# Fetching tile by tile with the second selection beside, and every second expert row summed on TensorE

## The chip, the cores and the metric

The kernel runs on one core of a Trainium2 chip. The metric is the device time of one execution in microseconds. A core has TensorE (PE), VectorE (DVE), ScalarE (ACT), GpSimd (POOL) and SyncE (SP), each with its own instruction stream; they meet by semaphores. DMAs are issued from SP's queue and from POOL's, and run on 16 DMA engines.

## The reference

Two blocks of two layers each on 256 tokens of width 1024. The change concerns the expert layer of the second block, which is called three times: in layer 0 for two streams of 256 tokens, in layer 1 for one.

```python
def _peer(h, wq, keys, u, v):              # per chunk of 128 tokens
    q = (hb @ wq).reshape(tc, 8, 2, 128)
    s = einsum('thpk,hpnk->thpn', q, keys)
    s_top, i_top = lax.top_k(s, 16)                    # per head and half: 16 of 128 keys
    cand = s_top[:, :, 0, :, None] + s_top[:, :, 1, None, :]
    cid = i_top[:, :, 0, :, None] * 128 + i_top[:, :, 1, None, :]
    best, pos = lax.top_k(cand.reshape(tc, 8, -1), 16) # 16 of 256 candidates per head
    eid = take_along_axis(cid.reshape(tc, 8, -1), pos, -1)
    g = softmax(best, -1)
    act = gelu(einsum('td,thed->the', hb, u[eid]))
    return einsum('the,thed->td', g * act, v[eid])
```

So each token chooses 8 x 16 = 128 experts out of 16384. Of each it needs one row of u (1024 floats) for a score and one row of v for the weighted sum. Before each layer the stream is scaled and shifted by vectors that come from `silu(c) @ w_mod`; those of layer 1 depend on nothing of layer 0.

## The kernel before

The program is written as stages, one behind the other, each with its own buffers and semaphores and an all-engine barrier at its end. The order inside a stage is written out by hand, engine by engine. An expert layer (`peer`, L1732) has these:

- scaling, `token_rows` (L1634) and `best_keys` (L1440): queries, key scores and the 16 best keys per head and half, for two tiles of 128 tokens (a token per partition).
- `select_experts` (L1544), once per tile: DVE forms the 256 candidates per head (`cand`, L1604), finds the 16 best by max, max_index and match_replace (`best16`, L1422), and turns positions into expert numbers through comparisons with 0 to 15 (`hit`, L1616 to L1620, twice). ACT does the exponentials (L1587). DVE ends with the weights (L1622 to L1625) and the index (L1628). Beside it, in layer 0 only, `Conditioning` (L502) computes a part of layer 1's scale and shift vectors: SP loads 1 MB pieces of `w_mod` into a ring of three (L521), PE multiplies (L539), ACT copies each group's row out (L527), PE turns the rows (L544), DVE adds the bias (L550). Three groups of two pieces go beside each selection, twelve groups in all.
- `gathered_experts` (L1654): POOL fetches for slot e and tile i one uv row per token (u and v side by side, 8 KB for each of 128 partitions, 1 MB in all) with an indirect DMA (L1676) into a ring of 12 buffers. The items alternate between the two tiles: 128 slots x 2 tiles = 256 fetches. They are worked off in batches of four. DVE multiplies and reduces the u half to a score (L1685), ACT applies gelu to four scores (L1721), DVE multiplies them by the weights (L1692), and then adds the four v halves, scaled by that number, to the tile's sum (L1699 for the first, L1703). The sums of a batch stand behind the scores of the next. A buffer is free when its sum is done (`s_summed`), and POOL waits for that before the fetch that reuses it. At the end PE turns both tiles' sums (L1728) and DVE adds them, gated, to x (L1715).

In what follows a fetch is one such item, and a stage's fetches are numbered from 0.

## Time and profile before

| | us |
|---|---|
| median of 3 runs | 4422.59 (4412.22 to 4424.36) |
| profiled execution, its own time | 4426.39 |
| its span in the trace | 4424.6 |
| DVE busy | 3183.9 (72%) |
| PE busy | 1744.0 (39%) |
| POOL busy | 1341.5 (30%) |
| ACT busy | 797.7 (18%) |
| DMA, software queue (the fetches) | 110592 packets, 805.36 MB |
| DMA, SP's queue | 58176 packets, 255.33 MB |

The profile comes from one execution. Its span leaves out 1.8 us of the execution's own time. Busy shares are means over very different stages: the three fetch stages run from 1712.9 to 2376, 2522.9 to 3186 and 3735.9 to 4398 us; PE is idle in them and busy in the stages between. A value in a fetch stage is therefore read from windows inside it. "Idle before, releaser" is the time in which the engine stood still ahead of an instruction, and what ended it.

### The profile page before, as it was taken

To read this page: it belongs to the slowest core of one execution; us is meant where nothing else is said; L and a number is where in the kernel's file an instruction comes from. 1 tells how busy PE (TensorE), PEld (TensorE's weight loads), DVE (VectorE), ACT (ScalarE), POOL (GpSimd) and SP (SyncE) were. 2 spreads that over 40 slices of the span, in tenths; PEclk is the share of its full clock that TensorE was granted. 3 is DMA by queue.
4 is the path that set the end of the run, shared out by engine and by line. 5 is a ranking of instruction groups with operands and counts; after the bars stand their busy time and mean duration, and the time that the engine had idled before them with its cause. 6 is when DMAs were issued, how large, how long until landed. Compare 5 with 4: busy or idle time off the path is not lost. (4 is left out here: it accounts for less than half of the span.)

```text
span 4424.6 us, 32217 instructions
## 1 busy us (share of the span) xinstructions
PE 1744.0 (39%) x9324; PEld 1322.3 (30%) x9324; DVE 3183.9 (72%) x5368; ACT 797.7 (18%) x1477; POOL 1341.5 (30%) x820
## 2 busy tenths in 40 slices
PE   6768975987877863000004500000166571000001
PEld 1657925954635650000004200000054471000001
DVE  3546545645264368999997799999843657999997
ACT  1335413522232230000002100000032240000000
POOL 0000000000000032666664166666300031666663
PEclk9868987998985786555556755555587885555555
DMA  7214452544100137999995499999630032999996
GB/s 285 80 38 151 162 228 100 176 168 174 56 0 1 38 122 286 421 419 418 417 419 210 186 422 422 418 418 415 261 125 0 1 124 87 422 422 419 419 418 251
DMA packets 168890, 1062.02 MB, mean 240 GB/s; under 512 B 18604, under 2 KB 22444, under 8 KB 57664
## 3 DMA queue, kind: packets, MB, share of 16 engines
q0 software_dynamic: 110592, 805.36, 43.9%
q1 hardware_dynamic: 58176, 255.33, 16.3%
q8 instruction: 41, 0.67, 0.1%
q14 instruction: 81, 0.66, 0.0%
HBM read 1059.56 MB, written 1.05 MB: 240 GB/s over the span
## 5 line engine op out<-in xcount | busy, mean ns | idle before, releaser
L1676 POOL DMA_INDIRECT peer_gather_raw<-in_peer_uv,peer_experts x768 | 1226.9, 1598 | 922.0 <-DVE peer_gather_out L1703 473.2
L1685 DVE CUSTOM_DVE_ANT_0 peer_gather_raw<-peer_gather_raw,peer_rows 128x1024 f32<-128x1024 f32 x768 | 912.0, 1223 | 122.8 <-DMA peer_gather_raw<-in_peer_uv,peer_experts 122.7
L1703 DVE SCALAR_TENSOR_TENSOR peer_gather_out<-peer_gather_raw,peer_gather_gelu,peer_gather_out 128x1024 f32<-128x1024 f32 x762 | 928.3, 1280 | 6.8
L1728 PE MATMUL peer_gather_acc<-all_constants,peer_gather_out 128*128 128x128 f32 x48 | 11.0, 424 | 2049.9 <-DVE peer_gather_out L1703 2049.9
L1540 POOL TENSOR_TENSOR peer_keys_lo<-peer_pick_wq_raw,peer_keys_hi 128x1024 fp32r<-128x1024 f32 x48 | 114.3, 2387 | 2107.5 <-ACT peer_keys_hi L1499 2107.5
L1728 PEld LDWEIGHTS peer_gather_acc<-all_constants,peer_gather_out 128*128 128x128 f32 x48 | 9.8, 227 | 2050.2 <-DVE peer_gather_out L1703 2050.2
L1721 ACT ACTIVATE peer_gather_gelu<-peer_gather_score 128x4 f32<-128x4 f32 x192 | 39.4, 205 | 1900.1 <-DVE peer_gather_score L1685 1900.1
L124 PE MATMUL ffn_up_acc<-first_h_hi,ffn_up_hi 128*128 128x256 f32 x704 | 202.1, 287 | 36.9 <-DVE ffn_up_lo L642 36.9
L124 PE MATMUL ffn_up_acc<-first_h_lo,ffn_up_hi 128*128 128x256 f32 x704 | 201.6, 286 | 0.0
L124 PE MATMUL ffn_up_acc<-first_h_hi,ffn_up_lo 128*128 128x256 f32 x704 | 201.5, 286 | 0.0
L452 PE MATMUL mod_acc<-mod_weights,mod_act_c 128*1 128x512 f32 (+1 forms) x288 | 142.0, 640 | 46.7 <-DMA mod_weights<-in_ada_w 32.9
L124 PEld LDWEIGHTS ffn_up_acc<-first_h_hi,ffn_up_hi 128*128 128x128 f32 x704 | 137.7, 196 | 37.7 <-DVE ffn_up_lo L642 37.7
L124 PEld LDWEIGHTS ffn_up_acc<-first_h_lo,ffn_up_hi 128*128 128x128 f32 x704 | 137.8, 196 | 0.0
L124 PEld LDWEIGHTS ffn_up_acc<-first_h_hi,ffn_up_lo 128*128 128x128 f32 x704 | 137.6, 196 | 0.0
L124 PE MATMUL peer_keys_acc<-peer_pick_hi,peer_keys_hi 128*128 128x256 f32 x384 | 115.5, 301 | 17.4 <-POOL peer_keys_lo L1540 17.4
L124 PE MATMUL peer_keys_acc<-peer_pick_lo,peer_keys_hi 128*128 128x256 f32 x384 | 111.4, 290 | 0.0
L124 PE MATMUL peer_keys_acc<-peer_pick_hi,peer_keys_lo 128*128 128x256 f32 x384 | 111.3, 290 | 0.0
L489 DVE SCALAR_TENSOR_TENSOR mod_part_sum<-mod_weights,mod_act_c,mod_part_sum 128x512 f32<-128x512 f32 x144 | 105.0, 750 | 3.8
L642 DVE TENSOR_TENSOR ffn_up_lo<-in_up_raw,ffn_up_hi 128x1024 fp32r<-128x1024 f32 x88 | 103.8, 1219 | 4.9 <-ACT ffn_up_hi L601 4.8
L539 PE MATMUL peer_select_next_acc<-peer_select_next_raw,peer_select_next_silu 128*2 128x512 f32 x192 | 90.1, 632 | 40.4 <-DMA peer_select_next_raw<-in_w_mod 40.4
L124 PE MATMUL ffn_down_acc<-ffn_hidden_hi,ffn_down_hi 128*128 128x256 f32 x352 | 101.6, 288 | 11.1 <-DVE ffn_down_lo L215 11.1
L124 PE MATMUL ffn_down_acc<-ffn_hidden_lo,ffn_down_hi 128*128 128x256 f32 x352 | 101.2, 287 | 0.0
(481 smaller groups left out, 4884.8 us busy)
## 6 DMA issues: line engine op xcount, KB each, us to landing
mod_weights<-in_ada_w SPq DMA_DIRECT2D x48, 1024.0 KB, 7.7
in_up_raw<-in_w_up SPq DMA_DIRECT2D x88, 512.0 KB, 4.1
mod_weights<-in_w_mod SPq DMA_DIRECT2D x24, 1024.0 KB, 6.2
peer_pick_wq_raw<-in_peer_wq SPq DMA_DIRECT2D x48, 512.0 KB, 3.5
peer_select_next_raw<-in_w_mod SPq DMA_DIRECT2D x24, 1024.0 KB, 5.8
...
peer_gather_raw<-in_peer_uv,peer_experts POOLq DMA_INDIRECT x768, 11.2
...
```

Of the source, the lines that this page charges most:

```text
L124: ins = nc.tensor.matmul(out, a, b, start=start and n == 0, stop=stop and n == 2, skip_group_check=True)
L452: ins = nc.tensor.matmul(acc[0:n, g % 2, :], act_c[:, k, :], wt[:, 2 * (g % 2), k, :], start=(k == 0), stop=False)
L489: ins = nc.vector.scalar_tensor_tensor(mine, wt[:, slot, k, :], scale, mine, ALU.mult, ALU.add)
L539: ins = nc.tensor.matmul(self.acc[0:n, g % 2, :], self.silu[:, i * KD // 2 + k, :], self.raw[:, u % 3, k, :], start=(i == 0 and k == 0), s ...
L642: nc.vector.tensor_tensor(w[1][:, slot, :], raw[:, slot, :], w[0][:, slot, :].bitcast(F32), ALU.subtract).then_inc(s_lo, 1)
L1540: nc.gpsimd.tensor_tensor(w[1][:, m % 4, :], raw[:, m % 4, :], w[0][:, m % 4, :].bitcast(F32), ALU.subtract).then_inc(s_lo, 1)
L1676: nc.gpsimd.indirect_dma_start(raw[:, n % ring].rearrange("p c d -> p (c d)"), None, uv_rows, bass.IndirectOffsetOnAxis(index[:, i, e:e + ...
L1685: nc.vector.tensor_tensor_reduce(raw[:, n % ring, 0, :], raw[:, n % ring, 0, :], rows[:, i, :], 1.0, 0.0, ALU.mult, ALU.add, score[:, e, i ...
L1703: nc.vector.scalar_tensor_tensor(out[:, i, :], raw[:, n % ring, 1, :], gelu[:, e, i:i + 1], out[:, i, :], ALU.mult, ALU.add).then_inc(s_su ...
L1721: nc.scalar.activation(flat(gelu, b), flat(score, b), ACT.Gelu).then_inc(s_gelu, 1)
L1728: ins = nc.tensor.transpose(acc[:, k, i * P:(i + 1) * P], out[:, i, k * P:(k + 1) * P], ident)
```

## The change

The two selections and the fetch stage become one stage, `fetched_experts`. Only the first tile's selection is done ahead of the fetches. The second tile's is a Python generator, `side`, of which DVE takes one step behind each of the first 20 scores. The fetches go tile by tile: 128 of tile 0, then 128 of tile 1. They are worked off in batches of two. The even fetch's v half is summed on PE: ACT writes a 128x128 diagonal with the token's factor (L1758), and PE multiplies it with the 1024 columns of v in two matmuls of 512 that accumulate in PSUM over the tile (L1792). The odd fetch's v half is summed on DVE as before (L1691, L1694). At the end of a tile DVE adds the two partial sums (`take`), PE turns the result (`turn`) and DVE adds it to x (`add`); for tile 0 this happens while tile 1's fetches run. POOL waits for PE's semaphore ahead of even fetches and for DVE's ahead of odd ones. `Conditioning` has six groups in place of three and runs once per stream instead of once per tile.

```diff
 class Conditioning:
-    GROUPS = 3
+    GROUPS = 6
...
+def fetched_experts(nc, name, rows, top, where, uv_rows, x, gate, iota, ident, upcoming=None):
+        batch, ring, dring = 2, 12, 4
+        per_tile = slots // batch
+        batches = NT * per_tile
+        n_of = lambda i, e: i * slots + e
...
             def _(pool):
-                for n, (e, i) in enumerate(items):
-                    if n >= ring:
-                        pool.wait_ge(s_summed, n - ring + 1)
...
+                for i in range(NT):
+                    pool.wait_ge(s_chosen, 2 * i + 1)
+                    for e in range(slots):
+                        n = n_of(i, e)
+                        if n >= ring:
+                            pool.wait_ge(s_summed if e % 2 == 0 else s_half, (n - ring) // 2 + 1)
+                        nc.gpsimd.indirect_dma_start(raw[:, n % ring].rearrange("p c d -> p (c d)"), None, uv_rows,
+                                                     bass.IndirectOffsetOnAxis(index[:, i, e:e + 1], 0)).then_inc(s_landed[n % ring], 16)
...
+                def select(tile):
...
+                    yield
+                    for h in range(PEER_H):
+                        step.done(nc.vector.max(best[:, h, 0:8], cand[:, h, :]))
+                        if h % 4 == 3:
+                            yield
+                    step.wait()
+                    for h in range(PEER_H):
+                        step.done(nc.vector.max_index(pos[:, h, 0:8], best[:, h, 0:8], cand[:, h, :]))
+                        step.done(nc.vector.match_replace(cand2[:, h, :], best[:, h, 0:8], cand[:, h, :], float(-3.4e38)))
+                        if h % 2 == 1:
+                            yield
...
+                    nc.vector.scalar_tensor_tensor(index[:, tile, :], pick[:, 0, :], float(N_KEYS), pick[:, 1, :],
+                                                   ALU.mult, ALU.add).then_inc(s_chosen, 1)
+                    dve.wait_ge(s_exp, 2 * tile + 2)
...
+                def accumulate(b):
+                    i, e = b // per_tile, b % per_tile * batch + 1
...
+                        dve.wait_ge(s_half, n // 2)
+                        nc.vector.scalar_tensor_tensor(odd[:], raw[:, n % ring, 1, :], gelu[:, i, e:e + 1], odd[:],
+                                                       ALU.mult, ALU.add).then_inc(s_half, 1)
+                def take(i):
+                    dve.wait_ge(s_half, (i + 1) * slots // 2)
+                    dve.wait_ge(s_summed, (i + 1) * slots // 2)
...
+                    nc.vector.tensor_tensor(out[:], summed[:, i].rearrange("p b c -> p (b c)"), odd[:], ALU.add).then_inc(s_out, 1)
+                def scores(b, side):
+                    i = b // per_tile
+                    for e in range(b % per_tile * batch, (b % per_tile + 1) * batch):
+                        if b and e % batch == 1:
+                            weigh(b - 1)
+                            accumulate(b - 1)
+                        n = n_of(i, e)
                         dve.wait_ge(s_landed[n % ring], 16 * (n // ring + 1))
...
+                        next(side, None)
...
+                for _ in select(0):
+                    pass
+                side = select(1)
+                scores(0, side)
                 for b in range(1, batches):
+                    scores(b, side)
+                    if b == 24 and beside:
+                        beside.vector(dve)
+                    if b == per_tile:
+                        take(0)
+                    if b == per_tile + 12:
+                        add(0)
...
             def _(act):
+                def spread(b):
+                    act.wait_ge(s_weighted, b + 1)
...
+                    nc.scalar.activation(diag[:, b % dring, :], ident, ACT.Copy, scale=gelu[:, i, e:e + 1]).then_inc(s_diag, 1)
+                if beside:
+                    beside.scalar(act, 0, 3)
+                exponentials(0)
+                if beside:
+                    beside.scalar(act, 3, beside.GROUPS)
+                activate(0)
+                for b in range(1, batches):
+                    activate(b)
+                    if b == 6:
+                        exponentials(1)
+                    spread(b - 1)
...
             def _(pe):
+                if beside:
+                    beside.tensor(pe)
                 for i in range(NT):
+                    for e in range(0, slots, 2):
+                        n = n_of(i, e)
+                        pe.wait_ge(s_diag, n // 2 + 1)
+                        for half in range(2):
+                            ins = nc.tensor.matmul(summed[:, i, half, :], diag[:, n // 2 % dring, :], raw[:, n % ring, 1, half * 512:(half + 1) * 512],
+                                                   start=(e == 0), stop=(e == slots - 2))
+                        ins.then_inc(s_summed, 1)
+                        if i and e == 16:
+                            turn(0)
```

Where the order changes, row by row. A semaphore is printed under the name of its first user in the program, so names such as `mod0_silu` say only that there is a wait. First VectorE (DVE) before, at the end of tile 1's selection in layer 0 and the start of the fetch stage:

```order
L1620 TENSOR_REDUCE peer_select_pick<-peer_select_hit 128x128 [waits mod0_silu]
L1622 TENSOR_REDUCE peer_select_total<-peer_select_best 128x8 [waits mod0_row,mod0_silu]
L1623 RECIPROCAL peer_select_total<-peer_select_total 128x8 [waits mod0_silu]
L1625 TENSOR_TENSOR peer_share<-peer_select_best,peer_select_total 128x128 [waits mod0_silu]
L1628 SCALAR_TENSOR_TENSOR peer_experts<-peer_select_pick 128x128
L550 TENSOR_TENSOR second_mods<-peer_select_next_cols,all_vectors 128x24 [waits swa_attention_out]
L556 TENSOR_SCALAR second_mods<-second_mods 128x8 [waits ffn0_up_silu]
L1565 UNCONDITIONAL_BRANCH
L1679 UNCONDITIONAL_BRANCH [waits barrier_Pool_Activation_PE_DVE_SP_release]
L1685 ISA peer_gather_raw,peer_gather_score<-peer_gather_raw,peer_rows 128x1024 [waits load_all_loaded]
L1685 ISA peer_gather_score 128x1
```

Here the scores (the custom instruction, L1685) stand behind both selections, behind the conditioning's two rows and behind a barrier.

VectorE now, at the end of tile 0's selection (the last pick is L1666, the index L1668, the weights L1671 to L1673):

```order
L1666 TENSOR_REDUCE peer_fetch_pick<-peer_fetch_hit 128x128 [waits mod0_joined]
L1668 SCALAR_TENSOR_TENSOR peer_fetch_experts<-peer_fetch_pick 128x128 [waits mod0_joined]
L1671 TENSOR_REDUCE peer_fetch_total<-peer_fetch_best 128x8 [waits swa_attention_back]
L1672 RECIPROCAL peer_fetch_total<-peer_fetch_total 128x8 [waits mod0_joined]
L1673 TENSOR_TENSOR peer_fetch_share<-peer_fetch_best,peer_fetch_total 128x128 [waits mod0_joined]
L1713 ISA peer_fetch_raw,peer_fetch_score<-peer_fetch_raw,peer_rows 128x1024 [waits load_all_loaded,swa_attention_out]
L1713 ISA peer_fetch_score 128x1
L1623 CAST peer_fetch_key_no<-peer_index 128x256
L1624 CAST peer_fetch_ranks<-all_constants 128x16
L1628 TENSOR_TENSOR peer_fetch_cand<-peer_top 128x2048
L1713 ISA peer_fetch_raw,peer_fetch_score<-peer_fetch_raw,peer_rows 128x1024 [waits mod0_loaded1,mod0_joined]
```

The index moved ahead of the weights; behind it comes the first score, and the rows of tile 1's selection (L1623 on) stand between the scores.

POOL before, from the end of the keys to the fetches:

```order
L1540 TENSOR_TENSOR peer_keys_lo<-peer_pick_wq_raw,peer_keys_hi 128x1024 [waits mod0_used] x16
L1457 UNCONDITIONAL_BRANCH
L49 ISA [waits barrier_Pool_Activation_PE_DVE_SP_gather] x4
L1671 UNCONDITIONAL_BRANCH [waits barrier_Pool_Activation_PE_DVE_SP_gather]
L1676 DMA peer_gather_raw<-in_peer_uv,peer_experts 128x2048 x12
L1676 DMA peer_gather_raw<-in_peer_uv,peer_experts 128x2048 [waits ffn0_up_silu] x244
```

POOL now:

```order
L1542 TENSOR_TENSOR peer_keys_lo<-peer_pick_wq_raw,peer_keys_hi 128x1024 [waits mod0_used] x16
L1459 UNCONDITIONAL_BRANCH
L49 ISA [waits barrier_Pool_Activation_PE_DVE_SP_gather] x2
L1605 UNCONDITIONAL_BRANCH [waits barrier_Pool_Activation_PE_DVE_SP_gather]
L1613 DMA peer_fetch_raw<-in_peer_uv,peer_fetch_experts 128x2048 [waits swa_attention_out]
L1613 DMA peer_fetch_raw<-in_peer_uv,peer_fetch_experts 128x2048 x11
L1613 DMA peer_fetch_raw<-in_peer_uv,peer_fetch_experts 128x2048 [waits peer00_fetch_summed]
L1613 DMA peer_fetch_raw<-in_peer_uv,peer_fetch_experts 128x2048 [waits peer00_fetch_half]
```

The first fetch waits for the index and for no barrier of the selections; later ones wait in turn for PE's and for DVE's sums.

ScalarE (ACT) now, from the conditioning to the first diagonals (L529 copies a group's row out, L1745 is the exponential, L1750 a gelu, L1758 a diagonal):

```order
L526 ACTIVATE peer_fetch_next_silu<-all_vectors 128x16
L529 ACTIVATE peer_fetch_next_rows<-peer_fetch_turned 2x512 [waits peer00_fetch_next_used] x3
L1745 ACT_TABLE_LOAD
L1745 ACTIVATE peer_fetch_best<-peer_fetch_best 128x128 [waits swa_attention_back]
L529 ACTIVATE peer_fetch_next_rows<-peer_fetch_turned 2x512 [waits peer00_fetch_next_used] x3
L1750 ACT_TABLE_LOAD
L1750 ACTIVATE peer_fetch_gelu<-peer_fetch_score 128x2 [waits ffn0_up_silu] x2
L1758 ACTIVATE peer_fetch_diag<-all_constants,peer_fetch_gelu 128x128 [waits ffn0_up_hidden_hi]
L1750 ACTIVATE peer_fetch_gelu<-peer_fetch_score 128x2 [waits ffn0_up_silu]
```

All six rows of the conditioning stand ahead of the first gelu; each diagonal stands behind the gelu of the next batch.

## Rows read from the trace of the kernel before

**Rows 1.** The page's costliest groups: busy us, mean ns, idle before and its releaser.

```profile
L1685 DVE CUSTOM_DVE_ANT_0 peer_gather_raw<-peer_gather_raw,peer_rows 128x1024 f32<-128x1024 f32 x768 | 912.0, 1223 | 122.8 <-DMA peer_gather_raw<-in_peer_uv,peer_experts 122.7
...
L1703 DVE SCALAR_TENSOR_TENSOR peer_gather_out<-peer_gather_raw,peer_gather_gelu,peer_gather_out 128x1024 f32<-128x1024 f32 x762 | 928.3, 1280 | 6.8
```

**Rows 2.** Windows: us, then busy of PE, PEld, DVE, ACT, POOL; clock, DMA share, GB/s.

```profile
1800.00:2300.00 500.00, 0.00 (x0) 0.00 (x0) 479.46 (x650) 10.27 (x50) 324.88 (x200) 0.50 1.01 419
```

**Rows 3.** Timeline of VectorE in mid-stage: start us, us, line, tiles, [idle <-releaser].

```profile
1806.37 1.22 DVE L1685 CUSTOM_DVE_ANT_0 peer_gather_raw<-peer_gather_raw,peer_rows 128x1024 f32<-128x1024 f32 x1 [0.31 <-DMA peer_gather_raw<-in_peer_uv,peer_experts]
...
1807.52 0.16 DVE L1692 TENSOR_TENSOR peer_gather_gelu<-peer_gather_gelu,peer_share 128x4 f32<-128x4 f32 x1
...
1816.33 1.23 DVE L1685 CUSTOM_DVE_ANT_0 peer_gather_raw<-peer_gather_raw,peer_rows 128x1024 f32<-128x1024 f32 x1 [0.23 <-DMA peer_gather_raw<-in_peer_uv,peer_experts]
```

**Rows 4.** Timeline of VectorE, first stage: first score, first products, 16th and last score.

```profile
1718.68 1.23 DVE L1685 CUSTOM_DVE_ANT_0 peer_gather_raw<-peer_gather_raw,peer_rows 128x1024 f32<-128x1024 f32 x1 [7.74 <-DMA peer_gather_raw<-in_peer_uv,peer_experts]
...
1738.08 1.42 DVE L1699 TENSOR_SCALAR peer_gather_out<-peer_gather_raw,peer_gather_gelu 128x1024 f32<-128x1024 f32 x2
...
1756.63 1.23 DVE L1685 CUSTOM_DVE_ANT_0 peer_gather_raw<-peer_gather_raw,peer_rows 128x1024 f32<-128x1024 f32 x1 [0.29 <-DMA peer_gather_raw<-in_peer_uv,peer_experts]
...
2358.80 1.23 DVE L1685 CUSTOM_DVE_ANT_0 peer_gather_raw<-peer_gather_raw,peer_rows 128x1024 f32<-128x1024 f32 x1 [0.24 <-DMA peer_gather_raw<-in_peer_uv,peer_experts]
```

**Rows 5.** Timeline of ScalarE, first selection of layer 0.

```profile
1672.93 0.59 ACT L527 ACTIVATE peer_select_next_rows<-peer_select_next_acc 2x512 f32<-2x512 f32 x1 [6.28 <-PE peer_select_next_acc L539]
...
1674.83 0.31 ACT L1587 ACTIVATE peer_select_best<-peer_select_best 128x128 f32<-128x128 f32 x1
```

**Rows 6.** TensorE: timeline of a conditioning, windows of it and of a layer norm.

```profile
1650.80 22.09 PE L539 MATMUL peer_select_next_acc<-peer_select_next_raw,peer_select_next_silu 128*2 128x512 f32 x48 [11.29 <-DMA peer_select_next_raw<-in_w_mod]
...
1660.00:1673.00 13.00, 12.89 (x31) 2.38 (x28) 12.72 (x27) 0.66 (x2) 0.00 (x0) 1.00 0.45 161
...
3187.00:3192.00 5.00, 4.81 (x6) 2.19 (x7) 0.00 (x0) 0.00 (x0) 0.00 (x0) 0.50 0.00 0
```

**Rows 7.** Timeline of POOL: the stage's first fetch and four later ones.

```profile
1712.88 1.09 POOL L1676 DMA_INDIRECT peer_gather_raw<-in_peer_uv,peer_experts  x1 [80.22 <-SPq L1670]
...
1992.69 2.65 POOL L1676 DMA_INDIRECT peer_gather_raw<-in_peer_uv,peer_experts  x1 [0.89 <-DVE peer_gather_out L1703]
...
2341.86 1.74 POOL L1676 DMA_INDIRECT peer_gather_raw<-in_peer_uv,peer_experts  x1 [2.38 <-DVE peer_gather_out L1703]
...
2343.90 0.94 POOL L1676 DMA_INDIRECT peer_gather_raw<-in_peer_uv,peer_experts  x1 [0.30 <-issue]
...
2345.15 1.98 POOL L1676 DMA_INDIRECT peer_gather_raw<-in_peer_uv,peer_experts  x1 [0.30 <-issue]
```

**Rows 8.** Timeline of VectorE, first selection of layer 0.

```profile
1645.95 0.29 DVE L1598 CAST peer_select_key_no<-peer_pick_index 128x256 bf16<-128x256 uint32 x1 [0.90 <-PEq L50]
...
1651.30 0.09 DVE L1429 MATCH_VALUE_LOAD peer_select_pos<-peer_select_best,peer_select_cand 128x8 f32 x1
...
1674.38 2.29 DVE L1620 TENSOR_REDUCE peer_select_pick<-peer_select_hit 128x128 f32<-128x2048 bf16 x1
...
1677.47 0.28 DVE L1628 SCALAR_TENSOR_TENSOR peer_experts<-peer_select_pick 128x128 uint32<-128x128 f32 x1
```

**Rows 9.** Timeline of the first stage's end.

```profile
2365.12 4.87 DVE L1703 SCALAR_TENSOR_TENSOR peer_gather_out<-peer_gather_raw,peer_gather_gelu,peer_gather_out 128x1024 f32<-128x1024 f32 x4
...
2368.86 3.68 PE L1728 MATMUL peer_gather_acc<-all_constants,peer_gather_out 128*128 128x128 f32 x16 [660.86 <-DVE peer_gather_out L1703]
...
2372.57 3.23 DVE L1715 SCALAR_TENSOR_TENSOR all_x<-peer_gather_acc,second_mods,all_x 128x256 f32<-128x256 f32 x8 [2.57 <-PE peer_gather_acc L1728]
```

**Rows 10.** Timeline of layer 1: first index, first fetch, last score.

```profile
3701.31 0.28 DVE L1628 SCALAR_TENSOR_TENSOR peer_experts<-peer_select_pick 128x128 uint32<-128x128 f32 x1
...
3735.92 0.95 POOL L1676 DMA_INDIRECT peer_gather_raw<-in_peer_uv,peer_experts  x1 [79.44 <-SPq L1670]
...
4380.59 1.23 DVE L1685 CUSTOM_DVE_ANT_0 peer_gather_raw<-peer_gather_raw,peer_rows 128x1024 f32<-128x1024 f32 x1 [0.24 <-DMA peer_gather_raw<-in_peer_uv,peer_experts]
```

274 lines of the change are left out of this document (129 added, 145 removed).

## The prediction

> **What bounds the kernel now.** I read the page's slices first: three stretches of about 640 us stand at some 420 GB/s with the DMA digit at 9, and they are the three fetch stages, 256 fetches of 1 MB each. The rest of the span is not touched. Then the costliest groups [rows 1]: VectorE (DVE) carries two passes over each fetch, the score (1223 ns) and the sum (1280 ns), and had only 122.8 us in all before its scores, all of it spent waiting for a DMA. That makes it look as if DVE were nearly the bound. The windows decide it [rows 2]: over 500 us in the middle of a stage the DMA share is 1.01 at 419 GB/s, while DVE is busy 479 of 500 us. The batch rows say the same [rows 3]: four scores and four sums repeat every 9.96 us (1806.37 to 1816.33), or 2.49 us per fetch, and in each period DVE waits 0.2 to 0.3 us for a fetch and not the other way round. Over a whole stage a fetch costs 2.509 us: from the 16th score at 1756.63 to the last at 2358.80 are 602.2 us for 240 fetches [rows 4]. So a fetch stage is bound by the DMA engines, with DVE about 3% behind them. Taking work off DVE there can't by itself shorten it. What can be shortened is the time in which the DMA engines carry no fetch: the second selection ahead of each stage, and the tail behind it.
>
> **The sum on VectorE and TensorE.** Half of the 1280 ns sums leave DVE. A pair of fetches then costs it two scores (pitch 1.15 to 1.2 us with the accumulator read), one sum (1.2) and one small product (0.2 [rows 3]): 3.8 us against 5.02 us of DMA. In its place ScalarE makes a diagonal per pair (128x128; the nearest row is the 128x128 exponential, 0.31 us [rows 5]), and TensorE does two f32 matmuls of 512 columns. Such a matmul stands in the trace as two records (24 matmuls per selection in the code, x48 in the row [rows 6]). At granted clock 1.00 (2.4 GHz) the window holds 31 records in 13 us, 0.42 each; at 0.50 (1.2 GHz) it holds 6 in 5 us, 0.83 each [rows 6]. A pair costs TensorE 1.7 us at the upper and 3.3 us at the lower level, below 5.02 in both. The clock was 0.50 through the middle of the stage before, with TensorE idle [rows 2]; I take 3.3 and keep 1.7 as the other end. Cost on the path: nothing in steady state, hidden by the DMA. The cover holds if slots come free in time. An even slot is held from its landing until its matmuls end: 3 fetches (7.5) to the second score behind it, 1.2 for that, 0.05 assumed for the hand-over, 0.21 for a gelu (10.27 us for 50 [rows 2]) and 0.31 on ScalarE, 3.3 on TensorE, together 12.6 us with rounding up. A new fetch needs 5.8 us from issue to landing (1712.88 [rows 7] to 1718.68 [rows 4]). That is 18.4 of the ring's 12 x 2.49 = 29.9 us, so 11 us are spare. The merge in the middle (DVE waits for the last pair's matmuls, 4 us, and adds for 1.3) fits into these 11, and so does the addition of tile 0 to x. The gain is nothing here, the loss nothing; what DVE's spare 1.2 us per pair pays for is the next part.
>
> **The start of the fetches.** Before, the first is issued at 1712.88, behind both selections. Now it needs only the first index. That is computed right behind the second pick (1674.38 + 2.29 = 1676.7 [rows 8]), before the weights: 1676.7 + 0.28 + 0.3 to issue = 1677.3. So the first fetch lands at 1683.1 and not at 1718.68, 35.6 us earlier. Against that stand three things.
> (a) All six conditioning groups now run in this stage, with loads that last about as long as before but reach into the fetches. TensorE consumes a group in 6.87 us (the 6.28 that ScalarE waits, and its copy) and had ended three at 1672.93 [rows 5]; loads are issued three units ahead, so about 2.5 of the 12 MB are still to come at 1677.3: 6 us of DMA time that the fetches do not get.
> (b) ScalarE serves these groups in order before its first gelu. The sixth ends at 1672.93 + 3 x 6.87 + 0.59 = 1694.1; a table load (1.3, the gap between the two ScalarE rows) and the gelu follow: 1695.6. With the shared DMA I take 1697. DVE has by then scored fetches 0 to 2 and done three steps of the second selection, and waits some 4 us for this gelu, with everything behind it.
> (c) The second selection costs DVE 31.8 us (1645.95 to 1677.75), of which 5.35 (to 1651.30) are done by 1697 [rows 8]. The other 26.4 lie between fetches 3 and 18. Up to the score of fetch 19 DVE has 17 scores x 1.2 = 20.4, nine sums with products 12.1 (the first is a plain product, 0.7 [rows 4]), and 26.4: 58.9 us, ending at 1756. Fetch 28 goes into the slot of fetch 16, freed 4.2 us later (those 3.9 and the hand-overs to TensorE and POOL, 0.3 assumed), and lands 5.8 us after that: 1697 + 68.9 = 1765.9. At the DMA's pace it would have landed at 1683.1 + 6 + 28 x 2.49 = 1758.8. For fetch 22 both times are equal to within a microsecond, so DVE is the bound for only about eight fetches: loss 7 us. Twelve buffers and DVE's lighter pairs hide the rest.
> From fetch 28 on the DMA is the bound again: 227 x 2.509 = 569.5, last landing 2335.4 against 2358.80, 23.4 us earlier. Stream 1 of the layer has the same program and lengths, 23.4 again. In layer 1 there is no conditioning: index 0.8 before its old place, as in layer 0 (1677.47 - 1676.7), 3701.31 - 0.8 = 3700.5; issue at 3701.1, first landing 3706.9, DVE goes on at once (three scores and three steps, 8.9 us), fetch 28 lands at 3715.8 + 68.9 = 3784.7 and the last at 4354.2 against 4380.59 [rows 10]: 26.4. Together 73 us.
> The steps of the selection could cost more between fetches than in one run: their bound below is the same 26.4, above it I know only that nothing of it is hidden (loss 26.4 in place of 7). I take the former, since both kinds of DVE operation wait for their own predecessor in the trace already.
>
> **The tail.** Before, 17.0 us pass from the last fetch (2358.80) to the end of the additions (2372.57 + 3.23) [rows 9], because two batches of four sums (4.87 each) still stand behind it. Now: score 1.2, gelu 0.3, diagonal of the pair before 0.3, then two pairs on TensorE 6.7, merge 1.3, eight transposes 1.9 (3.68 for 16), eight additions of half the width 2.2 (between 1.6 and the old 3.2): 14.1. That is 2.9 less at the lower clock, 6.2 less at the upper. I take 2.9: 9 us in three stages.
>
> **Sum.** 73 + 9 = 82 us off the profiled execution's 4426.4: 4344. That execution lies 3.8 us above the median of the timed runs; 4422.6 - 82 is 4341. I forecast 4342.
>
> **A rule against the change.** The software queue's fetches are written by POOL, and its instruction takes 0.94 us when it starts under a sum (2343.90) and 1.98 when a score starts with it (2345.15, the score at 2345.09) [rows 7], so DVE's operations do hold it up in this kernel. [...] If each fetch met one blocking operation, it would be the rival below.
>
> **Rivals.**
> 1. *Better: the upper clock and the undisturbed pace.* If TensorE, now busy two thirds of each pair, is granted 1.00, the tail gives 3.3 more per stage and slots come free 1.6 earlier (15 us in all). If deeper prefetching also takes the small irregularities out, a fetch costs 2.49 and not 2.509, 4.3 us per stage, 13 in all: 4314. For it: TensorE had 1.00 when it worked without pause [rows 6]. Against it: gaps of 1.7 us in each pair, and a DMA share of 1.01, which leaves little to smooth.
> 2. *The second selection is hidden less.* More waits between its steps, or a longer gelu stall: 10 us per stage lost on top, 4374; with nothing hidden 19 per stage, 4402. For it: DVE has no reserve at all between fetches 5 and 19. Against: the twelve-deep ring.
> 3. *Slower: POOL becomes the bound.* Every even fetch now wakes on TensorE's release, every odd one follows. A pair is free of cost up to 5.02 us. Woken fetches took 1.74, in one case 2.65, the others up to 1.98, with 0.30 between [rows 7]: 5.23 for the worst mixed pair, 5.90 for two of the worst. Halfway, 5.56, costs 0.54 x 113 pairs x 3 = 183 us: 4527. The change loses from 5.26 us per pair on. Against it: a usual pair is 1.74 + 1.98 + 0.6 = 4.3, and DVE is less busy than before.
> 4. *The fetches get slower by TensorE's reads or the new order.* Nothing in the trace shows it; at 2.60 us per fetch 4344 + 62 = 4406; from 2.62 on nothing is left.
>
> **How the numbers follow.** Forecast 57%, rival 1 16%, rival 2 14%, rival 3 8%, rival 4 5%. What a measurement of this kernel can tell from no change is 0.3%, 13 us. Forecast and rivals 1 and 2 are faster, with a fifth of rival 4: 88%; the rest of rival 4 is no change: 4%; slower 8%. The range goes from rival 1 with a little beyond (4308) to rival 2 without any cover (4395), leaving out rival 3, most of rival 4 and the edge of rival 2.
>
> **What would show it.** In the new profile: the first fetch of a stage 35 us after the first selection's start and not 67; a ScalarE gap with DVE waiting for a gelu near 1697 in layer 0, none in layer 1; DMA share below 1 for some 10 to 20 us around fetches 22 to 28 and 1.01 from there on at 415 to 422 GB/s; DVE waiting about 1.2 us for a DMA in every pair; matmul pairs of 3.3 us at clock 0.50, or 1.7 at 1.00; 14 us from the last fetch to the last addition. I would be wrong if POOL's pairs exceed 5.02 us, if the DMA share in the middle of a stage falls under 1, or if the selection's steps between fetches take clearly more than 26 us.

## The result, and the profile after

| | before | after |
|---|---|---|
| median of the timed runs, us | 4421.49 (4412.22 to 4424.36) | 4343.99 (4333.64 to 4348.36) |
| profiled execution / its span, us | 4426.39 / 4424.6 | 4342.01 / 4340.2 |
| the three expert layers together, us | 2424.7 | 2345.9 |
| the rest of the span, us | 1999.9 | 1994.3 |

The ratio is 0.9825, with a 95% interval of 0.9802 to 0.9848: 77 us less, where the prediction said 80 (4342). The rest of the span, which the change does not touch, moves by some us from run to run (1986.6 to 1993.2 in the experiments' profiles, e10 apart). The expert layers alone are the measure from here on, each from one profiled execution. Each is cut in three: A from the issue of SyncE's first load of the layer's query weights (1566.92 for the first one before, 1563.08 after) to the first score, B from the first score to the last, C from the last score to the end of the additions to x.

| us, stage 0 / stage 1 / layer 1 | A | B | C | sum of all |
|---|---|---|---|---|
| before | 151.8 / 151.1 / 150.9 | 640.1 / 640.7 / 639.2 | 17.0 / 17.0 / 17.0 | 2424.7 |
| after | 118.9 / 116.8 / 116.5 | 654.4 / 657.2 / 647.6 | 12.4 / 10.2 / 11.9 | 2345.9 |
| difference | -101.5 | +39.3 | -16.6 | -78.9 |
| forecast | -105.7 | +32.5 | -8.7 | -82 |

The forecast's row is the prediction's own terms sorted so: first landings 35.6, 35.6 and 34.5 earlier; last landing 652.3, 652.3 and 647.3 after the first; 2.9 per tail.

The page's costliest groups of the kernel after answer to [rows 1]:

```profile
L1792 PE MATMUL peer_fetch_summed<-peer_fetch_raw,peer_fetch_diag 128*128 128x512 f32 x1536 | 1108.4, 863 | 876.9 <-ACT peer_fetch_diag L1758 876.8
L1613 POOL DMA_INDIRECT peer_fetch_raw<-in_peer_uv,peer_fetch_experts x768 | 943.0, 1228 | 1117.5 <-PE peer_fetch_summed L1792 854.4
L1713 DVE CUSTOM_DVE_ANT_0 peer_fetch_raw<-peer_fetch_raw,peer_rows 128x1024 f32<-128x1024 f32 x768 | 936.4, 1222 | 420.6 <-DMA peer_fetch_raw<-in_peer_uv,peer_fetch_experts 420.1
...
L1694 DVE SCALAR_TENSOR_TENSOR peer_fetch_odd<-peer_fetch_raw,peer_fetch_gelu,peer_fetch_odd 128x1024 f32<-128x1024 f32 x378 | 485.9, 1285 | 13.5
```

DVE's scores now wait 420.6 us for a DMA in place of 122.8: it has the reserve. POOL waits for TensorE's release of a slot, as the code says, and its instruction got cheaper (1228 ns; before, the mean was 1598). Windows of the kernel after (columns as in [rows 2]), the middle of the first stage and then the stretch of its start where the DMA engines run dry:

```profile
1800.00:2300.00 500.00, 287.56 (x406) 91.72 (x407) 374.03 (x608) 49.66 (x200) 245.55 (x200) 0.77 1.01 422
```

```profile
1700.00:1720.00 20.00, 10.72 (x12) 2.91 (x12) 19.89 (x61) 1.49 (x6) 7.34 (x5) 0.74 1.01 422
1720.00:1740.00 20.00, 10.62 (x12) 3.17 (x12) 19.69 (x42) 4.36 (x9) 5.09 (x5) 0.62 0.95 381
1740.00:1760.00 20.00, 10.89 (x13) 3.63 (x13) 19.69 (x29) 1.98 (x8) 7.99 (x6) 0.67 0.82 304
1760.00:1780.00 20.00, 12.70 (x25) 4.47 (x24) 19.79 (x34) 2.48 (x10) 15.99 (x12) 0.94 0.92 362
```

In the middle DVE is busy 374 of 500 us, not 479, and the DMA share is 1.01 as before. In the three slices from 1720 on, DVE is busy without a pause (19.7 of 20) while the DMA engines carry 381, 304 and 362 GB/s: (422-381 + 422-304 + 422-362)/422 x 20 = 10.4 us of fetching are lost. That is the gap that term (c) of the prediction put at 7.

Steady state, timeline of TensorE, DVE and POOL (columns as in [rows 3]):

```profile
1851.19 3.61 PE L1792 MATMUL peer_fetch_summed<-peer_fetch_raw,peer_fetch_diag 128*128 128x512 f32 x4 [2.99 <-ACT peer_fetch_diag L1758]
1851.81 1.23 DVE L1713 CUSTOM_DVE_ANT_0 peer_fetch_raw<-peer_fetch_raw,peer_rows 128x1024 f32<-128x1024 f32 x1 [1.20 <-DMA peer_fetch_raw<-in_peer_uv,peer_fetch_experts]
...
1854.36 1.22 DVE L1713 CUSTOM_DVE_ANT_0 peer_fetch_raw<-peer_fetch_raw,peer_rows 128x1024 f32<-128x1024 f32 x1
1855.08 1.31 POOL L1613 DMA_INDIRECT peer_fetch_raw<-in_peer_uv,peer_fetch_experts  x1 [3.56 <-PE peer_fetch_summed L1792]
...
1856.16 1.99 PE L1792 MATMUL peer_fetch_summed<-peer_fetch_raw,peer_fetch_diag 128*128 128x512 f32 x4 [1.36 <-ACT peer_fetch_diag L1758]
1856.69 0.93 POOL L1613 DMA_INDIRECT peer_fetch_raw<-in_peer_uv,peer_fetch_experts  x1 [0.30 <-issue]
1856.78 1.23 DVE L1713 CUSTOM_DVE_ANT_0 peer_fetch_raw<-peer_fetch_raw,peer_rows 128x1024 f32<-128x1024 f32 x1 [1.20 <-DMA peer_fetch_raw<-in_peer_uv,peer_fetch_experts]
```

A pair repeats every 4.97 us (1851.81 to 1856.78), DVE waits 1.20 in each, POOL needs 2.54 for its two fetches (1855.08 to 1857.62), and TensorE's pair takes 3.61 once and 1.99 the next time: the clock goes back and forth between its two levels, 0.77 on average.

The start of the first stage, on POOL, DVE and ScalarE:

```profile
1673.86 1.08 POOL L1613 DMA_INDIRECT peer_fetch_raw<-in_peer_uv,peer_fetch_experts  x1 [45.05 <-DVE peer_fetch_experts L1668]
...
1681.98 1.23 DVE L1713 CUSTOM_DVE_ANT_0 peer_fetch_raw<-peer_fetch_raw,peer_rows 128x1024 f32<-128x1024 f32 x1 [7.64 <-DMA peer_fetch_raw<-in_peer_uv,peer_fetch_experts]
...
1684.79 0.59 ACT L529 ACTIVATE peer_fetch_next_rows<-peer_fetch_turned 2x512 f32<-2x512 f32 x1 [6.28 <-PE peer_fetch_turned L541]
1695.84 0.59 ACT L529 ACTIVATE peer_fetch_next_rows<-peer_fetch_turned 2x512 f32<-2x512 f32 x1 [10.46 <-PE peer_fetch_turned L541]
...
1697.74 0.20 ACT L1750 ACTIVATE peer_fetch_gelu<-peer_fetch_score 128x2 f32<-128x2 f32 x1
...
1697.97 0.16 DVE L1681 TENSOR_TENSOR peer_fetch_gelu<-peer_fetch_gelu,peer_fetch_share 128x2 f32<-128x2 f32 x1 [3.71 <-ACT peer_fetch_gelu L1750]
```

The stage began 3.4 us earlier in this execution (its first cast at 1642.52, against 1645.95 [rows 8]). The first fetch is issued 31.3 us behind that cast, as the working had it (1677.3 - 1645.95); before it was 67. It lands 8.1 us later, not 5.8. DVE then waits 3.71 us for the first gelu, forecast at some 4. The second stage of layer 0 has the same program and a longer wait, 6.20 us:

```profile
2466.77 1.23 DVE L1713 CUSTOM_DVE_ANT_0 peer_fetch_raw<-peer_fetch_raw,peer_rows 128x1024 f32<-128x1024 f32 x1 [6.05 <-DMA peer_fetch_raw<-in_peer_uv,peer_fetch_experts]
...
2485.36 0.16 DVE L1681 TENSOR_TENSOR peer_fetch_gelu<-peer_fetch_gelu,peer_fetch_share 128x2 f32<-128x2 f32 x1 [6.20 <-ACT peer_fetch_gelu L1750]
```

And the first stage's tail:

```profile
2336.36 1.22 DVE L1713 CUSTOM_DVE_ANT_0 peer_fetch_raw<-peer_fetch_raw,peer_rows 128x1024 f32<-128x1024 f32 x1
...
2338.17 5.89 PE L1792 MATMUL peer_fetch_summed<-peer_fetch_raw,peer_fetch_diag 128*128 128x512 f32 x8 [1.19 <-ACT peer_fetch_diag L1758]
...
2344.15 1.22 DVE L1702 TENSOR_TENSOR peer_fetch_out<-peer_fetch_summed,peer_fetch_odd 128x1024 f32<-128x1024 f32 x1 [4.82 <-PE peer_fetch_summed L1792]
2345.43 0.86 PEld L1782 LDWEIGHTS peer_fetch_turned<-all_constants,peer_fetch_out 128*128 128x128 f32 x8 [2.20 <-DVE peer_fetch_out L1702]
...
2346.57 2.16 DVE L1721 SCALAR_TENSOR_TENSOR all_x<-peer_fetch_turned,second_mods,all_x 128x128 f32<-128x128 f32 x8 [1.19 <-PE peer_fetch_turned L1782]
```

12.4 us from the last score to the end of the additions (2348.73), where 17.0 stood [rows 4, 9] and 14.1 was forecast.

**The pace, a trap in the windows.** The GB/s of the middle rose from 419 to 422, which looks like 0.7% on each fetch, 4 us per stage. It is no gain. From the 64th score (1854.36) to the last (2336.36) are 482.0 us for 192 fetches: 2.510 us, where before had 2.509 over 240 [rows 4]. In both traces eight fetches take 19.88 us, and every 30 to 40 fetches one of these stretches takes 0.95 longer. Where an expectation below takes a faster pace for granted, the count by scores does not bear it out.

### The profile page after: what moved, and what is told of

The parts are those of the page before. It is cut to its first block and busy times, and to the rows that moved or that the text cites. A ratio compares the mean times of both kernels' runs of the same rounds, so it can differ in the third digit from the quotient of the medians.

```text
span 4340.2 us, 36156 instructions
## 1 busy us (share of the span) xinstructions
PE 2835.8 (65%) x10860; PEld 1664.2 (38%) x10860; DVE 2773.7 (64%) x5202; ACT 950.9 (22%) x2053; POOL 1057.5 (24%) x820
## 5 line engine op out<-in xcount | busy, mean ns | idle before, releaser
L1792 PE MATMUL peer_fetch_summed<-peer_fetch_raw,peer_fetch_diag 128*128 128x512 f32 x1536 | 1108.4, 863 | 876.9 <-ACT peer_fetch_diag L1758 876.8
L1613 POOL DMA_INDIRECT peer_fetch_raw<-in_peer_uv,peer_fetch_experts x768 | 943.0, 1228 | 1117.5 <-PE peer_fetch_summed L1792 854.4
L1713 DVE CUSTOM_DVE_ANT_0 peer_fetch_raw<-peer_fetch_raw,peer_rows 128x1024 f32<-128x1024 f32 x768 | 936.4, 1222 | 420.6 <-DMA peer_fetch_raw<-in_peer_uv,peer_fetch_experts 420.1
L1792 PEld LDWEIGHTS peer_fetch_summed<-peer_fetch_raw,peer_fetch_diag 128*128 128x128 f32 x1536 | 348.9, 250 | 1631.0 <-ACT peer_fetch_diag L1758 1340.3
L1694 DVE SCALAR_TENSOR_TENSOR peer_fetch_odd<-peer_fetch_raw,peer_fetch_gelu,peer_fetch_odd 128x1024 f32<-128x1024 f32 x378 | 485.9, 1285 | 13.5
L1750 ACT ACTIVATE peer_fetch_gelu<-peer_fetch_score 128x2 f32<-128x2 f32 x384 | 78.1, 203 | 1747.7 <-DVE peer_fetch_score L1713 1747.7
L1758 ACT ACTIVATE peer_fetch_diag<-all_constants,peer_fetch_gelu 128x128 f32<-128x128 f32 x384 | 147.9, 386 | 0.4
L541 PE MATMUL peer_fetch_turned<-peer_fetch_next_raw,peer_fetch_next_silu 128*2 128x512 f32 x192 | 89.1, 625 | 32.2 <-DMA peer_fetch_next_raw<-in_w_mod 32.2
L489 DVE SCALAR_TENSOR_TENSOR mod_part_sum<-mod_weights,mod_act_c,mod_part_sum 128x512 f32<-128x512 f32 x144 | 105.0, 750 | 3.8
## 6 DMA issues: line engine op xcount, KB each, us to landing
peer_fetch_raw<-in_peer_uv,peer_fetch_experts POOLq DMA_INDIRECT x768, 17.5
```

Of the source, the lines that this page charges most:

```text
L489: ins = nc.vector.scalar_tensor_tensor(mine, wt[:, slot, k, :], scale, mine, ALU.mult, ALU.add)
L541: ins = nc.tensor.matmul(self.acc[0:n, g % 2, :], self.silu[:, i * KD // 2 + k, :], self.raw[:, u % self.RING, k, :], start=(i == 0 and k ...
L1613: nc.gpsimd.indirect_dma_start(raw[:, n % ring].rearrange("p c d -> p (c d)"), None, uv_rows, bass.IndirectOffsetOnAxis(index[:, i, e:e + ...
L1694: nc.vector.scalar_tensor_tensor(odd[:], raw[:, n % ring, 1, :], gelu[:, i, e:e + 1], odd[:], ALU.mult, ALU.add).then_inc(s_half, 1)
L1713: nc.vector.tensor_tensor_reduce(raw[:, n % ring, 0, :], raw[:, n % ring, 0, :], rows[:, i, :], 1.0, 0.0, ALU.mult, ALU.add, score[:, i, e ...
L1750: nc.scalar.activation(gelu[:, i, part], score[:, i, part], ACT.Gelu).then_inc(s_gelu, 1)
```

## The experiments

All are edits of the kernel after, but for e5. Differences are of A, B, C and the expert layers' sum, against before; the ratio is of the timed runs, with its interval.

| | A | B | C | sum | ratio to before |
|---|---|---|---|---|---|
| after | -101.5 | +39.3 | -16.6 | -78.9 | 0.9825 [0.9802, 0.9848] |
| e1 sums on DVE | -99.4 | +103.2 | -23.3 | -19.4 | 0.9934 [0.9917, 0.9951] |
| e2 selections ahead | -8.8 | +3.2 | -20.5 | -26.1 | 0.9951 [0.9935, 0.9968] |
| e3 step per pair | -99.5 | +13.7 | -17.5 | -103.4 | 0.9770 [0.9753, 0.9786] |
| e4 selection at once | -23.4 | -38.8 | -15.5 | -77.8 | 0.9809 [0.9773, 0.9845] |
| e5 before, batch 2 | -1.0 | +4.1 | -14.4 | -11.2 | 0.9945 [0.9924, 0.9965] |
| e6 gelu first | -100.4 | +29.7 | -14.0 | -84.7 | 0.9811 [0.9796, 0.9826] |
| e9 loads in the ring | -105.6 | +7.0 | -17.2 | -115.8 | 0.9734 [0.9710, 0.9759] |
| e10 all sums on PE | -105.0 | -1.2 | -10.3 | -116.6 | 0.9722 [0.9688, 0.9757] |
| e11 e1 and e3 together | -98.4 | +109.6 | -23.2 | -12.0 | 0.9966 [0.9944, 0.9988] |

The intervals of after, e4 and e6 overlap, and so do those of e3, e9 and e10 and those of e1, e2, e5 and e11. Between kernels of one such group the timed runs decide nothing; what is said of them rests on A, B and C of one profile each.

**e1: what is TensorE's half worth?** All sums on DVE, no diagonals and no sum matmuls; the selection stays between the fetches. The edit, shortened:

```diff
-    pool.wait_ge(s_summed if e % 2 == 0 else s_half, (n - ring) // 2 + 1)
+    pool.wait_ge(s_half, n - ring + 1)
...
+    for e in (both of the batch): nc.vector.scalar_tensor_tensor(odd[:], raw[...], ...)
```

> The changed kernel with one part taken back: both sums of each pair on VectorE, no diagonals and no matmuls; order of the fetches, selection beside them and conditioning stay. Theory A (VectorE's lighter pairs are needed to hide the second selection): a pair costs VectorE 4.9 us against 4.97 of DMA, so the 26 us of the selection are only caught by the ring (some 14 us of spare prefetch); DMA gap of 18 to 22 us per stage in place of about 9, and VectorE never catches up: 4344 + 30 to 50 = 4375 to 4395. Theory B (only the earlier start of the fetches counts, the sum on TensorE is worth nothing): within 5 us of 4344.

Measured: 4394.72 (4382.75 to 4396.29). The first score comes as early as in the kernel after, and then B is 103 us longer, all of A's gain: what was taken ahead of the fetches is paid again between them. Windows of e1, a piece of its first stage's start and its middle, and then its scores in that middle (us busy, mean ns | idle before them):

```profile
1730.00:1750.00 20.00, 0.00 (x0) 0.00 (x0) 19.72 (x21) 3.28 (x5) 8.74 (x4) 0.50 0.70 259
1750.00:1770.00 20.00, 0.00 (x0) 0.00 (x0) 19.32 (x29) 0.61 (x3) 10.48 (x6) 0.50 0.73 277
1850.00:2250.00 400.00, 1.97 (x8) 1.57 (x8) 394.32 (x565) 16.07 (x79) 301.76 (x160) 0.50 1.01 417
...
L1713 DVE CUSTOM_DVE_ANT_0 peer_fetch_raw<-peer_fetch_raw,peer_rows 128x1024 f32<-128x1024 f32 x159 | 188.1, 1219 | 0.0
```

DVE is busy 98.6% in the middle, and no score waits for its fetch any more (0.0 us of idle time in front of 159 scores; before, 16.1 in the same window). So VectorE, which takes 5.0 us per pair of fetches here (4.95 us of it work), sets the pace itself and can't make up the selection's 31.8 us. The last fetch of the first stage lands at 2340.2 and is scored only at 2354.58: of the 36.7 us that B grows by there, 22 are a later last landing and 14 are landed fetches that still wait for DVE. What e1 still gains is the shorter tail.

**e2: what is the selection's place worth?** Both selections, and both exponentials, before the first fetch or gelu; sums split as in the kernel after.

```diff
-    pool.wait_ge(s_chosen, 2 * i + 1)
+    pool.wait_ge(s_chosen, 2 * (NT - 1) + 1)
...
-    side = select(1)
+    for _ in select(1): pass
```

> The changed kernel, but both selections run ahead of the first fetch (the fetch queue waits for the second index); sums stay half on TensorE. Theory A (the gain is the earlier first fetch, minus what the selection holds up, plus the tail): first fetch about 33 us later than in the changed kernel, no gap behind it, tail 3 us and pace 5 us per stage better than before: 4395 to 4402. Rival C (taking sums off VectorE speeds the fetches themselves): close to 4344.

Measured: 4395.26 (4387.44 to 4405.59). DVE has its reserve (300 of 400 us busy in 1850:2250) and it brings nothing in B: +3.2. With e1, e5 and the kernel after this closes a square, in us of the three layers:

| | selections ahead | second one beside |
|---|---|---|
| sums on DVE | -11.2 (e5) | -19.4 (e1) |
| sums split | -26.1 (e2) | -78.9 (after) |

Counted from e5, the new place alone is worth 8.2 us, the split alone 14.9, and both together 67.7: 45 more than the two added up. The corner of e5 is not clean, since it keeps the old stages with their barriers and the alternating fetches; 7.8 of the 14.9 us lie in A, where no sum is done. The other two edges differ in one thing each: with the selection beside the fetches the split is worth 59.5 us (e1 to after), and with the sums split the place is worth 52.8 (e2 to after). By themselves TensorE's sums shorten next to nothing (B of e2), they pay for the selection.

**e3: are the steps too dense?** One step of the selection per pair of fetches in place of one per fetch (and the second exponential at pair 14, not 6). There are 19 steps, behind the first 19 scores in the kernel after.

```diff
-    next(side, None)
+    if e % batch == 1:
+        next(side, None)
```

> The changed kernel with the second selection's steps set behind every second score (one step per pair, over 40 fetches and not 20). Theory A (the gap around fetches 22 to 28 comes from VectorE's excess of 2.3 us per pair over the DMA): excess now about 0.3 us per pair, the ring takes it, gap gone: 7 to 10 us per stage, 4344 - 25 = 4319. Rival D (the gap comes from the conditioning's loads and the late gelu): at most 4 us in layer 0's two stages, 4336 to 4344.

Measured: 4316.73 (4309.86 to 4321.69), 24.5 us less than after in the layers. The gap is gone; two of the windows above, in e3:

```profile
1720.00:1740.00 20.00, 11.08 (x16) 3.70 (x16) 19.86 (x49) 1.98 (x8) 10.37 (x8) 0.83 1.01 420
1740.00:1760.00 20.00, 9.76 (x16) 3.70 (x16) 19.69 (x39) 1.98 (x8) 10.67 (x8) 0.84 1.01 420
```

B falls by 8.8, 11.4 and 5.5 in the three stages, 25.6 in all: this is the size of the gap, forecast as term (c) at 7, 7 and 8. In the second stage some 3 of the 11.4 are no gap: the kernel after got its first product 18.6 us behind the first score there, and e3 15.6. The selection's work is the same and DVE as busy. Only its density matters: at one step per pair the ring never runs out.

**e4: or all of it in one piece?** The second selection at once, and its exponential ahead of the first gelu, but after the first fetches are issued.

```diff
-    side = select(1)
+    for _ in select(1): pass
```

> The changed kernel, but the whole second selection runs between the first index and the first score, not in steps between scores; the fetches still start behind the first index. Theory A (twelve buffers hold 30 us of fetches, about as long as the selection's 32): the ring is full at about 36 us behind the first issue, the first release comes 5 us later, and from then on VectorE's pairs (3.8 us) are faster than the DMA's: gap about 5 us per stage in place of 9, and the late first gelu is covered too: 4325 to 4336. Rival E (the steps between scores are what hides the selection): gap of 26 us and more per stage, about 4390.

Measured: 4342.68 (4315.79 to 4348.44), above the expected 4336; the layers are 1.1 us from after: -4.2, +0.2 and +5.1 by stage. Its ring fills with 12 fetches while DVE selects (A only 23 shorter, B 39 shorter than before), and then the DMA engines stand dry for a while (1710 to 1730: share 0.74, 287 GB/s). Twelve slots are worth 12 x 2.5 = 30 us of cover against a selection of 31.8, and so the interleaving of the kernel after brings no more than its ring alone would.

**e5: the batch size alone**, in the kernel before.

```diff
-    batch, ring = 4, 12
+    batch, ring = 2, 12
```

> The kernel before with batches of two in place of four, nothing else. In the changed kernel a fetch costs 2.486 us over the stage, before 2.509. Theory H (the pace is lost because VectorE, 97% busy, has no reserve to absorb small delays): batches of two change nothing there and add a product (0.2 us) and a wait per pair, so VectorE needs 4.95 to 5.0 us per pair: pace 2.50 to 2.53 us, 4410 to 4435. Theory I (the pace is lost because slots are held too long in batches of four): held two fetches shorter, pace 2.486, about 5 us per stage off, and about 5 us less behind the last fetch: 4390 to 4400.

Measured: 4404.20 (4384.62 to 4407.10), between the two theories. Its windows show 422 GB/s too, its scores 2.516 us per fetch against 2.510: no gain of pace (B +4.1). What it gains is the tail, 17.0 to 12.2 us in each stage, because two batches of two sums are left behind the last score where two of four were. That is most of the 16.6 us that C gives in the kernel after; with e1's tail at 9.2, e2's at 10.2 and e10's at 13.6, TensorE's share makes the tail longer, not shorter.

**e6: the gelu's place.** ScalarE copies the sixth conditioning group behind the first gelus.

```diff
-    beside.scalar(act, 3, beside.GROUPS)
+    beside.scalar(act, 3, 5)
...
+    if b == 1 and beside:
+        beside.scalar(act, 5, beside.GROUPS)
```

> The changed kernel with ScalarE's order changed: the first two gelus and the first diagonal stand ahead of the copy of the conditioning's last group. Theory A (VectorE's start into the second selection is late by the stall for the first gelu, and each microsecond of it lengthens the gap behind): 3 to 4 us off each of layer 0's two stages, layer 1 as it is: 4336 to 4338. Rival J (the conditioning's loads, not the gelu, set the gap): no change, 4344.

Measured: 4337.10 (4334.10 to 4341.63). B is 4.2 and 6.2 us shorter in layer 0's two stages, where DVE had waited 3.71 and 6.20 us for the gelu, and 1.0 longer in layer 1, which has no conditioning. The layers as a whole take 5.0 and 3.2 us less and 2.4 more. ScalarE's first gelus now follow their scores (there was none until 1697.74 in the kernel after):

```profile
1684.33 0.20 ACT L1750 ACTIVATE peer_fetch_gelu<-peer_fetch_score 128x2 f32<-128x2 f32 x1 [1.80 <-DVE peer_fetch_score L1713]
1692.46 0.20 ACT L1750 ACTIVATE peer_fetch_gelu<-peer_fetch_score 128x2 f32<-128x2 f32 x1 [7.93 <-DVE peer_fetch_score L1713]
```

So term (b) stands: in these profiles the stall of layer 0 goes into B at its full length.

**e7 and e8: how much does the ring have to spare?** Six and eight slots in place of twelve.

```diff
-    batch, ring, dring = 2, 12, 4
+    batch, ring, dring = 2, 6, 4      (e8: 2, 8, 4)
```

> The changed kernel with a ring of 6 fetch buffers in place of 12. By the working of the prediction an even slot is busy for 18.4 us: held 12.6, then 5.8 from issue to landing. With twelve slots (29.8 us) that is hidden. With six the chain is the bound: held time shrinks with the wait for the DMA, so between (18.4 - 0)/6 = 3.07 us per fetch and 2.5: 3.07 gives 4344 + 0.58 x 750 = 4780. If the true chain is shorter than 15 us, nothing changes beyond a longer gap behind the selection (20 us per stage): 4400.

> The changed kernel with a ring of 8. With six buffers 5315 us were measured, 3.75 us per fetch: the slot's cycle holds three fetch periods p and 10.9 us of fixed time (hand-overs, matmuls at the lower clock, issue to landing), so p = 10.9/3 = 3.63 for six. For eight p = 10.9/5 = 2.18, below the DMA's 2.49: the pace stays 2.49 and only the gap behind the selection grows by the four buffers lost (up to 10 us per stage): 4344 to 4375. If instead the whole cycle of 22.5 us counts, p = 22.5/8 = 2.81: 4344 + 245 = 4590.

Measured, one run each: 5314.81 and 4522.24. Both expectations missed, to the same side. Windows of e7, then of e8, over 1850 to 2250:

```profile
1850.00:2250.00 400.00, 186.45 (x209) 58.27 (x210) 201.54 (x318) 26.31 (x106) 124.63 (x106) 0.61 0.75 274
```

```profile
1850.00:2250.00 400.00, 229.77 (x298) 72.10 (x296) 274.24 (x444) 36.20 (x146) 167.88 (x145) 0.69 0.98 380
```

By the scores 64 to 256 a fetch costs 3.80 and 2.74 us: a slot comes round in 6 x 3.80 = 22.8 and 8 x 2.74 = 21.9 us, not in 18.4. The prediction counted 5.8 us from issue to landing, but fetches are issued two at a time and share the engines: the median is 7.6 in e7 and 8.8 in e8. And the three fetches for which a slot waits behind its own last as long as the pace does, so a ring that is too small also lengthens the time for which its slots are held. Without these three fetches a cycle is 22.8 - 11.4 = 11.4 us in e7 and 21.9 - 8.2 = 13.7 in e8, where the prediction had 10.9. An estimate from these for a ring of twelve at 2.49 us: 18.9 to 21.2 of 29.9, so 9 to 11 us to spare, where 11 were forecast.

**e9: the conditioning loads.** On top of e3, the conditioning's loads go into the fetch ring, all twelve at once and early, and the first twelve fetches wait for their slots.

```diff
-    RING = 3
+    RING = 12
...
+    if n < ring and beside:
+        pool.wait_ge(beside.s_used, n + 1)
```

> One selection step per pair, and besides the conditioning's twelve 1 MB pieces are loaded at once into the twelve still empty fetch buffers (each fetch of the first round waits until TensorE has used the piece in its buffer). Theory A (the pieces still under way when the fetches start cost the fetches their own transfer time, 2.5 MB or 6 us per stage of layer 0, and nothing else of the start is left to gain): loads end about where the fetches begin: 4 to 6 us off each of layer 0's stages against the kernel with one step per pair (4317): 4305 to 4309. Rival K (the first twelve fetches, waiting for TensorE, start later and lose it again): 4317 or above.

Measured: 4303.89 (4285.77 to 4316.45). Against e3 the layers take 7.6, 3.0 and 1.8 us less, 12.4 in all; the last has no conditioning, so differences of 2 us between two profiles say nothing, and the interval overlaps e3's. What is clear is the order of events. The sixth group comes 17.6 us behind the issue of the first fetch (1670.69 in e9) and not 22.0, and the first gelu with it:

```profile
1688.25 0.59 ACT L529 ACTIVATE peer_fetch_next_rows<-peer_fetch_turned 2x512 f32<-2x512 f32 x1 [6.28 <-PE peer_fetch_turned L541]
...
1690.14 0.20 ACT L1754 ACTIVATE peer_fetch_gelu<-peer_fetch_score 128x2 f32<-128x2 f32 x1
```

**e10: does the other half of the sums matter, and what does the clock follow?** On top of e9, both sums on TensorE, a diagonal for each fetch (eight buffers for them in place of four).

```diff
-    for e in range(0, slots, 2):
+    for e in range(slots):
```

> The kernel with one selection step per pair and the conditioning's pieces in the fetch buffers, with the other half of the sums on TensorE too: one diagonal and two matmuls per fetch, none on VectorE. A pair then takes TensorE 3.4 us at granted clock 1.00 and 6.8 us at 0.50, against 4.97 us of DMA, and VectorE only 2.5. Theory F (the granted clock follows the work, since it rose already with half of it, to a mean of 0.77): clock near 0.9 to 1.0, fetches unhindered, nothing more to gain: 4304, with 2 to 4 us per stage either way for the tail. Theory G (TensorE stays at 0.50 for a good part): TensorE becomes the bound, up to 1.8 us per pair: 4304 + 690 = 4990 at the lower clock throughout, 4400 to 4600 for a mixture.

Measured: 4286.62 (4276.63 to 4307.44). In its profiled execution the attention stage, ahead of any changed code, was 22 us shorter than in e9's (window attention, 92.0 us for 113.9), so that much of its lead is not to be had from the change. The layers are: 2308.2 against e9's 2308.9. B gains 8 and C loses 7. The window 1850 to 2250 of e10:

```profile
1850.00:2250.00 400.00, 300.42 (x649) 117.78 (x648) 205.74 (x410) 63.21 (x240) 172.03 (x160) 0.99 1.01 422
```

TensorE is granted 0.99, where half the matmuls gave 0.77 and none 0.50. DVE falls to 51% and the fetches keep their pace, so the sum that the kernel after leaves on DVE costs nothing, and the clock goes with TensorE's own work.

**e11: is the spacing enough by itself?** All of e1's edit, and e3's:

```diff
+    if e % batch == 1:
+        next(side, None)
```

> Both sums on VectorE as in the first experiment, but one selection step per pair. Tells whether the wider spacing makes TensorE's share unnecessary. Theory A (VectorE has no reserve: 4.9 us per pair for sums and scores against 4.97, so the 26 us of the selection must come out of the ring's spare wherever they stand): same as the first experiment within 5 us, 4388 to 4400. Rival L (the spacing alone hides the selection): 4325 to 4345.

Measured: 4405.21 (4379.86 to 4408.21), the layers 7.4 us more than in e1, and a little above the expected 4400. Spread wider the steps cost as much: with no reserve on DVE a longer delay is not made up either. TensorE's half is what makes the spacing of e3 worth anything.

e3, e9 and e10 beat both kernels of the case: 4317, 4304 and 4287 against 4344 and 4421.

## Why the prediction was right

The mechanism held: the fetches start earlier, and the DMA engines bound the rest. That the total came within 2 us (4344 for 4342) is partly luck. The terms missed by 4.2 us (A), 6.8 (B) and 7.9 (C), the last in the other direction, so that 3 us were left of them in the layers; and the part of the span that the change does not touch was 5.6 us shorter in the profile after.

**The bound.** Right: 2.509 us per fetch by the DMA was used, 2.510 came. Moving the sums was to be worth nothing by itself, and e2's B says so. How near VectorE stood to being the bound shows in e1, where with all sums and the selection on it no score waits for a fetch.

**The start of the fetches.** -101.5 against -105.7. The issue was right to 0.1 us. The landing was 2.3 us late in the first stage, 8.1 us behind the issue and not 5.8: the conditioning loads were in front of the fetch as well as among the later ones. In e9, which has them loaded earlier, it takes 5.8, and layer 1, without conditioning, has -34.4 for -34.5.

**(a) and (b), loads and gelu.** B without the gap, which e3's B gives, is 5.5, 5.2 and 3.0 us longer than before; the forecast's was 5.2, 5.2 and 0. The 3.0 of layer 1 were not forecast, and what they are stays open (e2 has 1.5 there and e10 1.1). The gelu came at 1697.74, forecast 1697, but from a stage that began 3.4 earlier: ScalarE waited 10.46 us for the sixth group where it waits 6.28 for the others, while the first fetches were under way. The forecast had the first product 13.9 us behind the first landing (1697 - 1683.1); it came 16.0 us behind the first score in the first stage and 18.6 in the second. e6 sized the stall.

**(c), the selection between the fetches.** Mechanism and place right, the size too small: 25.6 us against 22, in layer 0 8.8 and 11.4 for 7 (10.4 by the DMA's own windows in stage 0), in layer 1 5.5 for 8. The chain itself was worked out well: from the first product to the landing of fetch 28 pass 67.7, 68.1 and 68.0 us where 68.9 stood. What was off in layer 0 is its beginning, the later gelu above. The slot's cycle (e7, e8) was off too, but the chain does not depend on it.

**The tail.** Too small in size, 16.6 for 8.7, and right in its reason, the fewer sums behind the last score. It was worked out at the lower clock. In stage 0, the last scores' matmuls took 5.89 for 6.7 and the transposes 1.10 for 1.9, with part of the matmuls and all transposes at the upper level; stage 1 has 10.2. The gain itself is the smaller batch, which e5 has without TensorE.

**The rivals.** 1: the faster pace did not come (2.510); the upper clock came for some pairs only. e10 has it throughout and gains 0.7 us in the layers, so in the steady state it is worth next to nothing. 2: nothing of the selection was left uncovered beyond the gap. 3: POOL's pairs take 2.5 to 3.0 us in the steady state and not 5.2. Its instruction takes 1228 ns in the mean where it took 1598 before, so the change relieved POOL. What it follows is open. The means are 1846 ns in e1 (DVE 98.6% busy), 1228 in the kernel after (75%) and 1095 in e10 (51%), which looks like DVE's busy share; but e5, with DVE 98% busy, has 1323, and before 96% went with 1598. One fetch of e5 starts right ahead of a score and takes 0.94 us, not the 1.98 of [rows 7]:

```profile
2004.18 0.94 POOL L1676 DMA_INDIRECT peer_gather_raw<-in_peer_uv,peer_experts  x1 [0.30 <-issue]
2004.21 1.22 DVE L1685 CUSTOM_DVE_ANT_0 peer_gather_raw<-peer_gather_raw,peer_rows 128x1024 f32<-128x1024 f32 x1
```

The Trainium skill (SBUF — State Buffer, "SBUF: two separate sides") has GpSimd wait for a port pair that DVE holds under a lock. Whether that is what lengthens the instruction here, no run shows. 4: no slower fetches with TensorE reading beside.

One figure of its list of signs was wrong against its own working: the first fetch was to be issued 31 us behind the selection's start, not 35.
